# A hybrid encoder layer on eight cores: channels on partitions throughout, 1024-token tiles, softmaxes with queries on partitions

## What is computed

```python
h = rms_norm(x, g_mix);  z = h @ w_in            # q k v | conv_u conv_B conv_C | gates
q, k = rope(q), rope(k)
y_attn = windowed_gqa_sink(q, k, v, sink) @ w_attn_out    # |i-j| <= 128, 8 q heads, 2 kv heads
y_conv = (cb * short_conv_centred(cc * cu, conv_w)) @ w_conv_out    # width 3
x = x + (g_a * y_attn + g_c * y_conv) @ w_o
x = x + memory_cross_attention(rms_norm(x, g_cross), rms_norm(mem, g_mem), w_cq, w_ckv, w_co)
hf = rms_norm(x, g_ffn)
x = x + (silu(hf @ w_gate) * (hf @ w_up)) @ w_down        # hidden width 5632
return rms_norm(x, g_final)
```

## Time and profile before

| | us |
|---|---|
| median of 3 runs | 3804.01 (3799.43 to 4315.42) |
| profiled execution, slowest core (core 5) | 8770.7 |
| profiled execution, core 7 | 3791.1 |
| profiled execution, core 6 | 3795.8 |
| profiled execution, cores 0 to 3 | 4065.7 to 4102.5 |

### The profile page before, as it was taken

One profiled execution on the slowest core, in us unless ns is written; L12 is line 12 of the kernel. 1 busy time (PEld: TensorE's weight loads), 2 busy tenths in 40 slices (PEclk: granted clock), 3 DMA queues, 4 the chain that ended last, 5 costly groups with the idle time before them and its releaser, 6 DMA issues.

```text
span 8770.7 us, 48483 instructions; the slowest of 8 cores (3791.1 to 8770.7 us)
## 1 busy us (share of the span) xinstructions
PE 8668.5 (99%) x18192; PEld 2928.3 (33%) x18192; DVE 957.6 (11%) x1360; ACT 730.4 (8%) x1324; POOL 520.2 (6%) x989
## 2 busy tenths in 40 slices
PE   7999999999999999999999999999999999999999
PEld 3432232222234322322222343333333443333332
DVE  1100010000021000100000211020000310110001
ACT  1100020000011000200000110020000110110000
POOL 0000000000000000000000000000000000000000
DMA  5333343333333333433333334444444434444443
GB/s 106 61 51 55 65 89 55 55 56 55 54 63 69 51 55 65 89 55 55 56 55 54 63 76 67 76 104 71 70 70 71 95 60 70 75 75 71 70 71 71
DMA packets 160019, 590.74 MB, mean 67 GB/s; under 512 B 17200, under 2 KB 17200, under 8 KB 152496
## 3 DMA queue, kind: packets, MB, share of 16 engines
q0 software_dynamic: 141840, 507.90, 35.7%
q1 hardware_dynamic: 17952, 79.73, 2.6%
HBM read 1078.62 MB, written 16.78 MB: 125 GB/s over the span
## 4 chain that ended last, share of the span: by engine, by line
PE 98%; ACT 1%; DVE 0%; DMA 0%; issue 0%; SPq 0%; ACTq 0%; DVEq 0%
PE ps L312 97%; PE ps L315 1%; ACT arena L327 1%; DVE arena L341 0%; DMA arena<-x 0%; DVE arena L330 0%; DMA out<-arena 0%; SPq L353 0%; ACTq L137 0%; DVE arena L441 0%; ACT L327 0%; DVEq L137 0%; SPq L137 0%
## 5 line engine op out<-in xcount | busy, mean ns | idle before, releaser
L312 PE MATMUL ps<-arena 128*128 128x512 bf16 (+2 forms) x17296 | 8550.9, 721 | 6.7 <-DVE arena L330 4.4
L312 PEld LDWEIGHTS ps<-arena 128*128 128x128 bf16 x17296 | 2819.1, 163 | 5706.0 <-issue 5433.1
L330 DVE TENSOR_TENSOR arena<-ps,arena 128x512 f32<-128x512 f32 (+5 forms) x1008 | 650.2, 666 | 7615.7 <-PE ps L312 7344.0
L353 POOL DMA_DIRECT2D arena<-wp x984 | 519.3, 528 | 8187.6 <-PE ps L312 8117.4
L327 ACT ACTIVATE arena<-ps 128x512 f32<-128x512 f32 (+4 forms) x538 | 336.6, 648 | 4787.9 <-PE ps L312 4759.0
L327 ACT ACTIVATE arena<-arena 128x512 bf16<-128x512 f32 (+4 forms) x419 | 262.4, 627 | 1359.4 <-DVE arena L330 1310.8
L341 DVE SCALAR_TENSOR_TENSOR arena<-arena 128x1024 bf16<-128x1024 f32 (+2 forms) x192 | 223.7, 1193 | 140.3 <-ACT arena L327 132.5
L327 ACT ACTIVATE arena<-ps,arena 128x512 f32<-128x512 f32 x128 | 88.0, 687 | 1473.8 <-PE ps L312 1473.8
L315 PE MATMUL ps<-arena 128*128 128x128 bf16 x896 | 130.7, 354 | 73.9 <-DVE arena L341 73.6
L315 PEld LDWEIGHTS ps<-arena 128*128 128x128 bf16 x896 | 110.1, 157 | 113.9 <-issue 107.2
L330 DVE TENSOR_TENSOR arena<-arena 128x512 bf16<-128x512 f32 (+2 forms) x124 | 77.4, 624 | 17.2 <-ACT arena L327 4.6
## 6 DMA issues: line engine op xcount, KB each, us to landing
arena<-wp POOLq DMA_DIRECT2D x920, 512.0 KB, 5.3
arena<-x SPq DMA_DIRECT2D x38, 1024.0 KB, 13.0
arena<-wp POOLq DMA_DIRECT2D x64, 384.0 KB, 4.9
arena<-gv SPq DMA_DIRECT2D x17, 1024.0 KB, 7.8
out<-arena SPq DMA_DIRECT2D x16, 1024.0 KB, 4.1
arena<-cs SPq DMA_DIRECT2D x8, 384.0 KB, 7.7
arena<-mem SPq DMA_DIRECT2D x2, 1024.0 KB, 10.6
arena<-cst POOLq DMA_DIRECT2D x1, 320.0 KB, 8.9
```

Source lines behind the costliest of these rows:

```text
L312: pr.add("pe", lambda e: e.matmul(out, lhsT, rhs, start=start, stop=stop), reads=[lhsT, rhs], writes=[out])
L330: pr.add("dve", lambda e: e.tensor_tensor(out, in0, in1, op), reads=[in0, in1], writes=[out])
L353: return pr.add(q, lambda e: e.dma_start(out=out, in_=in_), reads=list(sb_reads), writes=list(sb_writes), is_dma=True)
```

## The change

- x, mem and the result lie in HBM with channels as rows (the host transposes), and the residual `xT` lies so in SBUF. No activation is transposed any more. A norm needs a sum over partitions: ScalarE squares a 128x512 chunk, VectorE adds it to `acc` (`square_acc`), 16 chunks make a half tile, and one f32 matmul with ones gives the sum over partitions in every partition (`finish_rstd`). Ln and Exp on ScalarE give `rstd`, and `norm_chunk` (VectorE, one for each of 16 chunks) the normed half. At the start of the first tile the squares go straight through f32 matmuls.
- Two tiles of 1024 tokens, in halves of 512 (`hf`). Each weight piece is loaded once for two tiles instead of four, and most loops (`proj2`) use a piece for both halves. The last w_down group, and the first half's q and k at the start, run the halves one after the other and load their pieces twice. The FFN has three groups of 15, 15 and 14 blocks.
- k and v are kept for the whole sequence; the halo is one block, computed once, in the first tile. In it the conv's neighbour column takes matmuls of one column, 256 in all.
- Both softmaxes have queries on partitions: scores of a block and a head are 128 queries by 384 (cross: 256) keys, VectorE adds the mask and takes the maximum, ScalarE exponentiates with the sum on the side, VectorE multiplies by the reciprocal, TensorE transposes the probabilities, ScalarE copies them out, and then P times V. `at` spreads the steps of 16 units over the conv rounds: scores in one slot, transposes two slots on, P times V three slots on.
- x is read again for the residual (`out_proj`), and twice more for the next tile's norm, in 128x512 chunks (`xload`, four buffers `xr`); finished chunks are stored in the same loop.

```diff
 D = 2048
 S = 2048
-T = 512
+T = 1024
 NT = S // T
-EXT = T + 256
+HW = 512
...
 NFB = DFF // 128
-FG = 4
-FGB = NFB // FG
+FGROUPS = (15, 15, 14)
 EPS = 1e-6
...
+        def square_acc(src, dst, first, n=HW):
+            if first:
+                act(dst, src, AF.Square)
+            else:
+                s = sq[:, sqn[0] % 2, 0:n]
+                sqn[0] += 1
+                act(s, src, AF.Square)
+                tt(dst, dst, s, ALU.add)
+
+        def finish_rstd(src, dst, n=HW):
+            b = balloc()
+            mm(bank(b)[:, 0:n], onesF, src, True, True)
+            act(dst, bank(b)[:, 0:n], AF.Ln, bias=epsb, scale=1.0 / D)
+            act(dst, dst, AF.Exp, scale=-0.5)
+            bfree(b)
+
+        def norm_chunk(dst, src, gi, c, r):
+            stt(dst, src, gains[gi][:, c:c + 1], r, ALU.mult, ALU.mult)
+
...
+            s = sq[:, c % 2, :]
+            act(s, xT[:, 0, c, :], AF.Square)
+            mm(bank(b0), onesF, s, c == 0, c == 15)
+        act(rstd[:, 0, :], bank(b0), AF.Ln, bias=epsb, scale=1.0 / D)
+        act(rstd[:, 0, :], rstd[:, 0, :], AF.Exp, scale=-0.5)
+        bfree(b0)
+        for c in range(16):
...
+            def score(u):
+                n, g = u // 2, u % 2
+                kbs, m0 = keys(n)
+                nk = 128 * len(kbs)
+                sl = u % 2; s4 = u % 4
+                for h in range(4):
+                    b = balloc()
+                    mm(bank(b)[:, 0:nk], qT[:, n, 4 * g + h, :], kT[:, g, kbs[0] * 128:kbs[0] * 128 + nk], True, True)
+                    tt(Sb[:, sl, h, 0:nk], bank(b)[:, 0:nk], mask[:, m0:m0 + nk], ALU.add)
+                    bfree(b)
+                rmax(st_mx[:, s4, :], Sb[:, sl, :, 0:nk])
+                tt(st_mx[:, s4, :], st_mx[:, s4, :], sinkS[:, 4 * g:4 * g + 4], ALU.max)
+                ts(st_ng[:, s4, :], st_mx[:, s4, :], float(-SCALE), ALU.mult)
+                tt(st_es[:, s4, :], sink[:, 4 * g:4 * g + 4], st_ng[:, s4, :], ALU.add)
+                for h in range(4):
+                    act(Sb[:, sl, h, 0:nk], Sb[:, sl, h, 0:nk], AF.Exp, bias=st_ng[:, s4, h:h + 1], scale=SCALE,
+                        accum=st_l[:, s4, h:h + 1])
+                act(st_es[:, s4, :], st_es[:, s4, :], AF.Exp)
+                tt(st_l[:, s4, :], st_l[:, s4, :], st_es[:, s4, :], ALU.add)
+                recip(st_r[:, s4, :], st_l[:, s4, :])
+                for h in range(4):
+                    ts(Pb[:, sl, h, 0:nk], Sb[:, sl, h, 0:nk], st_r[:, s4, h:h + 1], ALU.mult)
+
...
+                bfree(b)
+
+            at = {}
+            for u in range(16):
+                s = (27 * u) // 20
+                at.setdefault(s, []).append((2, score, u))
+                at.setdefault(s + 2, []).append((1, turn, u))
+                at.setdefault(s + 3, []).append((0, pv, u))
...
+        def resid(b, c, hf, first, stats=True):
+            x = xT[:, hf, c, :]
+            tt(x, bank(b), x, ALU.add)
+            bfree(b)
+            if stats:
+                square_acc(x, acc[:, hf, :], first)
+
+        def out_proj(it):
+            for c in range(16):
+                for hf in range(2):
+                    dma_x(xT[:, hf, c, :], c, T * it + hf * HW, HW)
+            for c in range(12):
+                b = proj2(wF(("o", c)), lambda hf: lambda k: mT[:, hf, k, :])
+                for hf in range(2):
+                    resid(b[hf], c, hf, c == 0)
+            ws = [wF(("o", c)) for c in range(12, 16)]
+            for hf in range(2):
+                for c in range(12, 16):
+                    b = proj(ws[c - 12], lambda k: mT[:, hf, k, :])
+                    resid(b, c, hf, False)
+                if hf == 0:
+                    finish_rstd(acc[:, 0, :], rstd[:, 0, :])
+                    for c in range(16):
+                        norm_chunk(hT[:, 0, c, :], xT[:, 0, c, :], 1, c, rstd[:, 0, :])
+
...
+            def score(n):
+                hf, nn = n // 4, n % 4
+                sl = n % 2; s4 = n % 4
+                bs = [balloc(), balloc()]
+                for h in range(4):
+                    o = (h % 2) * NMEM
+                    mm(bank(bs[h // 2])[:, o:o + NMEM], qcT[:, h, hf, nn * 128:(nn + 1) * 128], KmT[:, h, :], True, True)
+                for p in range(2):
+                    rmax(st_mx[:, s4, 2 * p:2 * p + 2], bank(bs[p]).rearrange("p (a b) -> p a b", b=NMEM))
+                ts(st_ng[:, s4, :], st_mx[:, s4, :], float(-SCALE), ALU.mult)
+                for h in range(4):
+                    o = (h % 2) * NMEM
+                    act(Ec[:, sl, h, :], bank(bs[h // 2])[:, o:o + NMEM], AF.Exp, bias=st_ng[:, s4, h:h + 1], scale=SCALE,
+                        accum=st_l[:, s4, h:h + 1])
+                bfree(bs[0]); bfree(bs[1])
...
+            def pv(hf):
+                for h in range(4):
+                    b = balloc()
+                    for j in range(2):
+                        mm(bank(b), Vm[:, j, h * 128:(h + 1) * 128], PTc[:, h, j, :], j == 0, j == 1)
+                    act(qcT[:, h, hf, :], bank(b), AF.Copy)
+                    bfree(b)
+
+            def co(hf, cs):
+                for c in cs:
+                    b = balloc()
+                    for k in range(4):
+                        mm(bank(b), wc[c // 4][:, c % 4, k * 128:(k + 1) * 128], qcT[:, k, hf, :], k == 0, k == 3)
+                    resid(b, c, hf, c == 0)
+
+            wq = [wF(("cq", h)) for h in range(4)]
+            cq(0)
+            finish_rstd(acc[:, 1, :], rstd[:, 1, :])
+            for c in range(16):
+                norm_chunk(hT[:, 1, c, :], xT[:, 1, c, :], 1, c, rstd[:, 1, :])
+            score(0); score(1)
+            cq(1)
...
+            pv(0)
+            co(0, range(0, 4))
+            turn(4); score(6)
+            co(0, range(4, 8))
+            turn(5); score(7)
+            co(0, range(8, 12))
+            turn(6)
+            co(0, range(12, 16))
+            turn(7)
+            finish_rstd(acc[:, 0, :], rstd[:, 0, :])
+            for c in range(4):
+                norm_chunk(hT[:, 0, c, :], xT[:, 0, c, :], 2, c, rstd[:, 0, :])
+            pv(1)
+            for q in range(4):
+                co(1, range(4 * q, 4 * q + 4))
+                if q < 3:
+                    for c in range(4 + 4 * q, 8 + 4 * q):
+                        norm_chunk(hT[:, 0, c, :], xT[:, 0, c, :], 2, c, rstd[:, 0, :])
+
...
+                def xload(c, hf):
+                    s = xr[:, xn[0] % 4, :]
+                    xn[0] += 1
+                    dma_x(s, c, t1 + hf * HW, HW)
+                    return s
+
+                def final_chunk(hf, c):
+                    o = xT[:, hf, c, :]
+                    norm_chunk(o, o, 3, c, rstd[:, hf, :])
+                    out_dmas.append(dma("sp", out_d[c * 128:(c + 1) * 128, T * it + hf * HW:T * it + (hf + 1) * HW], o, sb_reads=[o]))
+
+                for hf in range(2):
+                    for c in range(16):
+                        b = proj(wF(("down", fg, c)), lambda k: aT[:, k, hf, :], KC=nb)
+                        resid(b, c, hf, c == 0)
+                        if hf == 1:
+                            final_chunk(0, c)
+                        if not last:
+                            if hf == 0:
+                                square_acc(xload(c, 0), nacc[:, 0, :], c == 0)
+                                if c >= 8:
+                                    square_acc(xload(2 * c - 16, 1), nacc[:, 1, :], c == 8)
+                                    square_acc(xload(2 * c - 15, 1), nacc[:, 1, :], False)
+                                if c == 15:
+                                    for i in range(2):
+                                        finish_rstd(nacc[:, i, :], nrstd[:, i, :])
+                            else:
+                                for i in range(2):
+                                    norm_chunk(hT[:, i, c, :], xload(c, i), 0, c, nrstd[:, i, :])
+                    finish_rstd(acc[:, hf, :], rstd[:, hf, :])
+                if last:
+                    for c in range(16):
+                        final_chunk(1, c)
+                else:
+                    load_cs(it + 1)
+                    for i in range(8):
+                        finals.append(lambda i=i: (final_chunk(1, 2 * i), final_chunk(1, 2 * i + 1)))
+            return finals
+
+        nacc = view(c_lo, F32, (2, HW))
+        nrstd = view(c_lo + 4096, F32, (2, HW))
```

1039 lines of the change are left out of this document (456 added, 583 removed).

## The result

The changed kernel takes 3957.6 us (median; 3956.7 to 3957.9 in the runs that compare), the kernel before 3799 to 3804 in the same comparison: ratio 1.0409, 95% interval 1.0388 to 1.0429. It is slower by 4.1%, where 2.0% was forecast: on the right side of no change, but twice the size, inside the wide range of 3780 to 3970 and 28 us above the forecast's own range of 3835 to 3930. Repeated later beside the experiments it was 3952 to 3962.

A forecast was written before the change was run, and what follows sets the result against it. TensorE's columns, then serial passages, were taken to bound the kernel before. Terms -90 + 15 + 17 + 2 + 17 + 112 + 4 = +77 gave 3868 on core 7's scale, 3881 median; own range 3835 to 3930, wide range 3780 to 3970.

The forecast's parts named there:

- two slots of distance allow a lag of about 8: Attention beside the conv: lag allowed between scores and P times V, giving 15 lost in the second tile, 2 in the first.
- Columns, -90: Whole program: 415.5 fewer units of 512 matmul columns at 0.2168 us each, -90 us.
- One-column matmuls and f32, +15 and 3 to 7: 256 one-column matmuls at 0.061 us each, +15; f32 matmuls 3 to 7 us, counted inside other terms.
- The head, +17: Start of the first tile: attention starts near 187 us, 86 to 87 lost against 70 before, +17.
- 16 x 0.9 us: Head: time on VectorE for the second half's square sums, 16 chunks of 0.9 us.
- Norm passages, +2: From w_o's first half into the FFN: 94.5 lost a tile, 189 for two, against 186 before, +2.
- Attention, +17: Attention beside the conv: VectorE needs 191 us against TensorE's 168; 15 lost in the second tile, 2 in the first.
- The change of tiles, +112: Last w_down group: gated loads of x make second-half rounds 9.0 us against 3.03; with 20 in the first half, +112.
- The step "4.0 us" for the landing: Change of tiles: VectorE's wait for a 256 KB load of x each round, ends 2.3 and 4.8.
- The first (loads don't gate): Change of tiles: with free landings the term falls from 112 to about 45, time to 3814; chance 0.17.
- The third (passages shrink): Norm passages: a tile loses 50 instead of 94.5; with the first rival 3705 to 3790; chance 0.10.
- The second, longer chains: Passages and attention slots: VectorE's chains longer than walked, 30% more cost, +70, 3950 us; chance 0.18.

The follow-up runs named there:

- x10: Changed kernel with self-attention's transposes and P times V one slot later, and four slots instead of two for squares in the head: 3955 us.
- x3: Changed kernel with the addition of a square to its running sum issued one chunk later on VectorE: 3916 to 3930 us, ratio 1.0294.
- x4: Changed kernel with reciprocal and scaling of a self-attention unit issued one slot later: 3921 to 3925 us, ratio 1.0296.
- x5: Changed kernel without the maximum in either softmax: 3865 to 3867 us, ratio 1.0145.
- x2: Changed kernel with the next tile's square sums taken in the middle FFN group: 3962 to 3963 us, ratio 1.0403.
- x1: Changed kernel with the loads of x at the change of tiles issued one round ahead of the store: 3956 to 3957 us, ratio 1.0387.
- x7: Changed kernel with early square sums and loads of x one round ahead together: 3916 to 3919 us, ratio 1.0284.
- x9: x7 with eight slots for x instead of four and loads three rounds ahead: 3880 to 3912 us, ratio 1.0227.

## Where the prediction was right, and which steps failed

The forecast named the right places and the right sign, but +77 where +165 was measured. Two steps failed. In the attention stages, the step from VectorE's work to lost time ("two slots of distance allow a lag of about 8", so that only the sum counts) gave 32 us of loss where 76 were measured. At the change of tiles the mechanism held and the term was mis-sized, 112 for 156: landings beside the refill of weights, 7.9 us where 4.0 was taken, were left out, above all in the first half (40 us lost where 20 was forecast). A smaller one is the head's square sums, 0.9 us a chunk for 1.51.

**Columns, -90.** Right. The rate is 0.2158 us per 512 columns, not 0.2168. The 460 us of the earlier trace rows, with 457.86 busy, begin with nine matmuls that start 0.42 us apart, before the clock is full (granted 0.78 between 3311 and 3320 us), and these make the 2 us by which the mean came out too high.

**One-column matmuls and f32, +15 and 3 to 7.** The 256 one-column matmuls were 8.7 us in all (34 ns each in busy time; a single one is 163 ns to its end and overlaps the next), so the upper bound of 15 was too high. The f32 ones were too cheap: each matmul of 512 columns with f32 operands is two instructions (62 for 31), 45.5 us in all.

```profile
L304 PE MATMUL ps<-arena 128*128 128x512 f32 x62 | 45.5, 850 | 194.5 <-DVE arena L322 170.9 <-ACT arena L319 23.5
...
L304 PE MATMUL ps<-arena 128*128 128x1 bf16 x256 | 8.7, 163 | 0.0
```

What one costs depends on the granted clock, as two stretches of the head show, the first with one f32 matmul at 0.50, the second with two at 1.00:

```profile
26.00:29.00 3.00, 2.05 (x2) 0.50 (x2) 0.00 (x0) 0.00 (x0) 0.00 (x0) 0.50 1.01 176
...
40.30:42.50 2.20, 1.96 (x4) 0.57 (x4) 0.00 (x0) 1.32 (x3) 0.00 (x0) 1.00 1.02 322
```

From one start to the next an f32 instruction takes 0.43 us at 1.00 and 0.85 at 0.50, so a matmul takes 0.86 and 1.7. The Trainium skill ("FP8 and Floating Point Precision", section "TensorE Precision Notes") has four passes; the trace agrees, 0.86 at the full clock against 0.2158. The 15 of 512 columns that nothing hides are busy 23 us against the 3 to 7 of the forecast, spread over head, passages, change of tiles and end: half the statistics stand behind a long wait and run at 0.50.

**The head, +17.** Mis-sized: it is +37. The step that failed is "16 x 0.9 us" for the second half's square sums. The two slots make it 1.51 a chunk, and x10 takes 9 us off by four slots. Attention thus starts at 207 and not 187, which the forecast had named as a sign of being wrong. The other 11 or so (waits for norm chunks between ropes, the memory norm, f32 statistics) were not tried apart.

**Norm passages, +2.** Right in mechanism, and 17 us too long: walked to 202 us each, they took 195 and 191, and lose 172 against 189. (Against the 203 of before this is -31; 17 of the difference to +2 come from the rate, by which before loses 203 and not 186.) The 2.2 us of the residual chain is 2.17 in the trace, and x3 shows that it is the handoff to ScalarE and back that counts: 0.97 of the 2.17 went, with no instruction less.

**Attention, +17.** This term failed: beside the 8.7 us of one-column matmuls the two stages lose 67. The chain on VectorE was not the error, 9.06 us measured against 9.8 walked. The step that failed is the one that turned it into time: "15 units in 20 slots", "two slots of distance allow a lag of about 8", and so only the sum of VectorE's work counted. VectorE's work is in order and holds other engines' resources meanwhile: a PSUM bank of the convolution waits behind a unit's chain, and TensorE behind the bank. x10 gives the distance more and gains 11 to 14; x4 lets the bank go in the middle of the chain, with no work left out, and gains 35; x5 shortens the chain by a quarter and gains 58. So the longest stretch for which VectorE is held counts for more than the distance between scores and use: about half of the 67 by x4. The further 23 of x5 can come from a shorter hold or from less work in all; no run tells these two apart.

**The change of tiles, +112.** Right in mechanism, too small by 44. It is 39 + 117 instead of 20 + 92. The step "4.0 us" for the landing was right for the quiet part, and wrong where weights refill:

```profile
arena<-xT SPq DMA_DIRECT2D x28, 256.0 KB, 7.9
...
arena<-xT SPq DMA_DIRECT2D x30, 256.0 KB, 4.0
```

The first row is 1850 to 1937 us (DMA share 0.88), the second 1937 to 2102 (share 0.55), both from the view of DMA issues. In the first half the forecast counted VectorE's surplus and three loads, but not that these landings are twice as long there: rounds of 3.0 to 3.7 us while there is one load in each, then, with three, 9.2, 12.3, 14.2 and 7.8, before they settle at 4.5 to 4.9. x2 measures the half's loss at 41 where 20 was forecast. In the second half the last thirteen rounds take 7.8 to 12.7 us, 9.2 on the mean, where 9.0 was forecast; the three before take 10.9, 10.4 and 22.8, while weights are refilled. The rule of the Trainium skill that was weighed there ("DMA: Bandwidth & Descriptors", section "Anatomy of one DMA — SWDGE (gpsimd) path") gave rounds of 7.6 us and 90 for the term; the trace is on the other side. x1 and x2 together (x7) take off 86, and x9 shows that most of the rest is the DMA engines' time, with VectorE's chain of 4.2 us a round as the floor under it.

**The end, +4.** +8; of it nothing was tried by itself.

**The rivals.** The first (loads don't gate) is excluded by x1. The third (passages shrink) didn't occur, though x3 shows that some 23 us a tile of it are there to be had. The second, longer chains, gave nearly the measured time, 3950, by luck: the chains are no longer than walked (9.06 us for 9.8, 2.17 for 2.2) and the passages came out shorter, and it is what stands behind the chains in attention and the loads at the change of tiles that were priced too low. Its remark that the clock would be lower in longer waits came true, 0.80 and 0.83 in the passages against 0.90.

So the sum's excess of 88 us over the forecast's 77 is 44 (change of tiles) + 44 (attention) + 20 (head) + 4 (end) + 9 (second tile's q and the remainder) - 33 (passages, -31 where +2 was forecast) = 88.

## What to carry to other kernels

When work moves to an engine that executes in order, size it by the longest stretch that it holds the engine without a break, and ask whose buffer or bank is freed behind that stretch; its sum over the stage tells too little. A handoff to another engine and back inside a loop is worth moving one iteration later wherever the buffers allow it (with two slots they may not). And a load that is issued behind a store or a result of the same round costs its landing time every round, which near a refill of weights was twice what it was in a quiet place.

## What the runs showed of the hardware

- A matmul with f32 operands of 512 columns runs as two instructions. At a granted clock of 1.00 each takes 0.43 us from start to start, 0.86 together, four times the bf16 one's 0.2158; at 0.50 each takes 0.85. So a lone one behind a long wait costs about twice what it costs in dense work.
- A one-column bf16 matmul costs TensorE 34 ns of busy time with its weight load (256 in 8.7 us), below the 61 ns of a pair with 128 columns.
- The same 256 KB load landed in 4.0 us at a DMA share of 0.55, 7.9 at 0.88 and 19.6 when more were in flight at 0.9 and above. Weights took 6.2 us of all DMA engines per MB, x and results 3.3, as in the rows of before (3.2 us for a piece of half a MB, 3.04 for a MB). The MB are of what is written; a weight is read as f32, twice that, so per MB read the two cost about the same.
- From VectorE to ScalarE and back is 0.88 us for a square of 0.63: each handoff is about 0.1 to 0.15 us.
